# A Vector product moved behind a weight step, and the column split of one down-projection matmul regrouped

## The reference

```
x = x + 0.5 * rms(swiglu(rms(x)))                       # ffn1, d_ff = 2816
x = x + rms(mix(diff_attention, ssd) @ w_mix_out)       # two branches, gated
x = x + rms(cross_attention(x, mem))
x = x + 0.5 * rms(swiglu(rms(x)))                       # ffn2, d_ff = 2816
# second block
proj = rms(x) @ w_in_2
v, x1, x2 = split(short_conv(hy_in))
for o, gate in enumerate((x1, x2)):                     # hyena: long convolution by FFT
    zc = gate * (irfft(rfft(zc) * k_spec[o]) + bias * zc)
attn = softmax(q k / sqrt(96)) v                        # 8 heads, no mask
x = x + (g_hy * (zc * silu(z_hy)) @ w_hy_out + g_at * (attn * silu(z_attn)) @ w_attn_out) @ w_out
```

## Time and profile before

| | |
|---|---|
| runs of the kernel before | 1109.22, 1107.14, 1108.89 us |
| median | 1108.89 us |
| profiled execution | 1109.22 us, of which the span is 1107.4 us |
| PE busy | 1091.7 us, 99% of the span, 8538 matmuls |
| DVE busy | 792.8 us, 72% |
| ACT busy | 590.7 us, 53% |
| PEclk, all 40 slices | 9, which is 90% or more |

### The profile page before, as it was taken

One profiled execution on the slowest core, in us unless ns is written; L12 is line 12 of the kernel. 1 busy time (PEld: TensorE's weight loads), 2 busy tenths in 40 slices (PEclk: granted clock), 3 DMA queues, 4 the chain that ended last, 5 costly groups with the idle time before them and its releaser, 6 DMA issues.

```text
span 1107.4 us, 21002 instructions
## 1 busy us (share of the span) xinstructions
PE 1091.7 (99%) x8538; PEld 1035.5 (94%) x8538; DVE 792.8 (72%) x1112; ACT 590.7 (53%) x844; POOL 0.2 (0%) x4
## 2 busy tenths in 40 slices
PE   9999999999999999999999999999999999999998
PEld 8999999999999999999999888899999798999998
DVE  6765556858898977777777867665555686997774
ACT  5444444567764335587744555454444575655561
POOL 0000000000000000000000000000000000000000
PEclk9999999999999999999999999999999999999999
DMA  8665555455444336444555434365556445543341
GB/s 302 245 224 189 201 183 189 184 191 178 167 157 148 97 132 205 158 152 153 190 175 182 171 115 160 101 224 192 189 187 206 136 167 200 187 152 118 112 153 38
DMA packets 29137, 188.59 MB, mean 170 GB/s; under 512 B 3496, under 2 KB 4809, under 8 KB 7370
## 3 DMA queue, kind: packets, MB, share of 16 engines
q1 hardware_dynamic: 26592, 181.42, 47.4%
q10 hardware_dynamic: 2474, 6.15, 1.7%
HBM read 186.50 MB, written 1.05 MB: 169 GB/s over the span
## 4 chain that ended last, share of the span: by engine, by line
PE 80%; DVE 13%; ACT 4%; issue 2%; DMA 1%; ACTq 0%; SPq 0%; DVEq 0%
PE bank L508 23%; PE bank L510 23%; PE bank L509 23%; DVE sb_w_lo L1990 3%; PE bank L589 2%; DVE sb_ssd_conv L2213 2%; ACT sb_w_hi L1304 2%; PE bank L833 1%; PE bank L715 1%; PE bank L663 1%; DVE sb_hT_lo L2067 1%; DMA sb_w_raw<-in_w 1%; PE bank L1151 1%; PE bank L1050 0%; PE bank L978 0%
## 5 line engine op out<-in xcount | busy, mean ns | idle before, releaser
L1990 DVE TENSOR_TENSOR sb_w_lo<-sb_w_raw,sb_w_hi 128x2048 fp32r<-128x2048 f32 x169 | 386.4, 2290 | 153.2 <-ACT sb_w_hi L1304 153.0
L508 PE MATMUL bank<-sb_hT_hi,sb_w_hi 128*128 128x256 f32 x1560 | 440.3, 282 | 2.0 <-DVE sb_hT_lo L2067 1.0
L509 PE MATMUL bank<-sb_hT_lo,sb_w_hi 128*128 128x256 f32 x1560 | 433.1, 278 | 0.0
L510 PE MATMUL bank<-sb_hT_hi,sb_w_lo 128*128 128x256 f32 x1560 | 433.0, 278 | 0.0
L1304 ACT ACTIVATE sb_w_hi<-sb_w_raw 128x2048 fp32r<-128x2048 f32 x169 | 322.7, 1910 | 35.5 <-PE bank L510 34.1
L508 PEld LDWEIGHTS bank<-sb_hT_hi,sb_w_hi 128*128 128x128 f32 x1560 | 293.4, 188 | 6.0 <-issue 4.3
L509 PEld LDWEIGHTS bank<-sb_hT_lo,sb_w_hi 128*128 128x128 f32 x1560 | 292.9, 188 | 1.5 <-issue 1.2
L510 PEld LDWEIGHTS bank<-sb_hT_hi,sb_w_lo 128*128 128x128 f32 x1560 | 292.5, 188 | 0.0
L1358 ACT ACTIVATE sb_ffn_gate<-sb_ffn_gate 128x256 f32<-128x256 f32 x44 | 18.4, 418 | 137.2 <-DVE sb_ffn_gate L2082 137.1
L508 PE MATMUL bank<-sb_w_hi,sb_hT_hi 128*128 128x256 f32 x256 | 73.4, 287 | 0.6 <-DVE sb_hT_lo L2742 0.2
L510 PE MATMUL bank<-sb_w_hi,sb_hT_lo 128*128 128x256 f32 x256 | 71.3, 279 | 0.0
(11 more groups left out here) (437 smaller groups left out, 1801.5 us busy)
## 6 DMA issues: line engine op xcount, KB each, us to landing
sb_w_raw<-in_w SPq DMA_DIRECT2D x169, 1024.0 KB, 5.0
sb_x<-in_x SPq DMA_DIRECT2D x2, 512.0 KB, 4.4
sb_w_raw<-in_w SPq DMA_DIRECT2D x4, 256.0 KB, 6.5
sb_w_raw<-in_w SPq DMA_DIRECT2D x2, 512.0 KB, 7.7
sb_mem_xn<-in_mem ACTq DMA_DIRECT2D x1, 1024.0 KB, 7.1
sb_post_g<-in_ffn_post_g ACTq DMA_DIRECT2D x2, 512.0 KB, 4.5
sb_decay<-in_c_decay ACTq DMA_DIRECT2D x1, 768.0 KB, 4.4
out<-sb_x SPq DMA_DIRECT2D x3, 256.0 KB, 2.1
```

The source lines that it names most:

```text
L508: pe.matmul(o, a_hi, b_hi, start=first, stop=False)
L509: pe.matmul(o, a_hi, b_lo, start=False, stop=False)
L510: return pe.matmul(o, a_lo, b_hi, start=False, stop=last)
L1990: tt(w_lo[b % STAGES][:], w_raw[b % RING][:], f32(w_hi[b % STAGES][:]), ALU.subtract).then_inc(w_lo_in, 1)
```

## The change

The entry of `LAST_DOWN` for the eight looped down blocks of ffn2 changes from two pieces of 256 columns in all three products to pieces of 320 and 192 columns in the third product alone. And on DVE `hyena_product(0, 1)` moves from the tail of step 0, where it stood between `softmax_rows(0)` and `low_after`, to the head of step 1, which is behind the `low_after` of step 0 and ahead of `softmax_rows(1)`.

```diff
 LAST_DOWN = {1: (((256, 256), False), ((256, 256), True), ((384, 128), False)),
-             2: (((256, 256), True), ((256, 256), True), ((448, 64), False))}
+             2: (((256, 256), True), ((320, 192), False), ((448, 64), False))}
...
                 if i == 0:
                     hyena_product(0, 0)
                     centred_conv(4)
+                elif i == 1:
+                    hyena_product(0, 1)
                 elif i == 3:
...
                     softmax_rows(i)
                 if i in (4, 6, 8):
                     at_low(c)
-                if i == 0:
-                    hyena_product(0, 1)
-                elif i == 1:
+                if i == 1:
                     centred_conv(5)
```

## The result

| | before | after |
|---|---|---|
| median | 1109.22 us (5 runs, 1107.14 to 1110.63) | 1115.08 us (5 runs, 1113.50 to 1116.57) |
| ratio after / before, 95% interval | | 1.0054, 1.0039 to 1.0069 |
| profiled execution, its span | 1109.22 us, 1107.4 us | 1114.64 us, 1112.8 us |

A forecast was written before the change was run, and what follows sets the result against it. PE, busy 99% of the span, was taken as the bound. The wait's +2.78 us and the split's -0.1 made +2.7: 1111.6 us on the median, put at 1111.5 for new runs, range 1109.7 to 1112.8 for 8 in 10.

The forecast's parts named there:

- Part two, the wait: Product moved behind step 0's `w_lo` on DVE: PE waits at the transposes of head 1, +2.78 us (2.4 to 3.15).
- six steps: Chain from `softmax_rows(0)`: DVE idles 3.15 us for `w_hi`, row maximum and ACT's exponentials shift 3.15, PE ends 2.78 us late.
- second wait: Further PE wait behind the transposes, at `hyena_back(0)`: worth 0 to 0.37 us, taken as nothing.
- the step after the sixth: `hyena_unfold(0)` now ends at 1012.94, PE wants its second half at 1013.02: fits by 0.08 us, less the hop.
- Part one, the split: ffn2's looped down blocks, third product in 320 + 192: 0.01 us saved a turn, eight turns -0.1 us (-0.2 to +0.2).
- The four shapes: Down-block splits in the trace: all three 256 + 256, third alone 256 + 256, 384 + 128 or 448 + 64; excess 0.03 to 0.11 us.
- The excess of 0.05: Old split, all three products 256 + 256: 1.18 us from first L715 matmul to fifth up-block start, against ideally 1.13.
- The rival on the clock: PE's clock falls to 1.2 GHz behind the gap at the transposes: 2.7 us more, 1114.3 us; chance 0.06.
- the wait of 1.89 us: PE's longest idle time in the trace before, which left the clock at 1.00; cited against the clock falling.
- half a weight block at half rate: Clock rival's price: 24 matmuls of 256 columns behind the gap take 0.227 us instead of 0.113, costing 2.7 us more.

## Why the prediction was wrong in size

**Part two, the wait: right.** Its six steps hold one by one. 2.78 us was forecast; at full clock the move alone costs 2.94 by its mean and 2.5 in its profile, and in the profile after it was 3.10. There DVE stood some 0.36 us later against PE than the forecast had it (`w_lo` at 997.64 is 1.14 behind it, PE just ahead of the place 0.78), which would make up the difference. No second wait came in `hyena_back(0)`, as the step after the sixth says.

**Part one, the split: the price at the cut was right, and the sum that followed from it was wrong.** The step that failed is the one that closed the account at the fifth matmul: "Nothing hides it, since PE is the bound in the loop, and nothing else depends on it." What depended on it was the pitch of the 96 matmuls behind. The four shapes were each read for 1.2 us, and each of them happens to be followed by the fast pitch, so no view of the shapes at the cut could tell. But the trace had it. The excess of 0.05 that the prediction gives the old cut was this very thing in part: from 752.24 to 752.71 the matmuls of 256 columns take 0.118 each, and 0.113 from there on. Whoever had asked where in the whole trace 256 columns take 0.118 would have found two states, 136 of 452 stretches in the slow one, and a loop of 768 matmuls in the fast one that the change could push over. That risk is 768 x 0.0045 = 3.5 us, less what the first matmuls behind each cut paid before, and it had no place among the rivals. It was forecast at -0.1 and is +3.1 in the trace, +3.5 in the runs of the split alone.

The Trainium skill ("TensorE: Matmul & The Clock Gate", section "Back-to-back issue gap") gives an isolated matmul N / 2.4 + 2.5 ns, by an estimate 109 ns for 256 columns. The matmuls here are not isolated, each has its own weight load; in a long stream the traces have 113.3 or 117.8 ns, and no run here shows 109.

**The rival on the clock: the mechanism was real, its chance and price were not.** It had a chance of 0.06 and +2.7 us. It came in 9 of 14 executions that had this wait, and cost 1.5 us. The argument against it, the wait of 1.89 us that leaves the clock at 1.00, was one case, and with three operations moved, where the new wait is 1.22 us, 4 of 11 executions lost the clock. The forecast needed both numbers: how often, and that the half clock lasts 3.4 us (PE was busy for 3.29 of them), where it had taken half a weight block at half rate, 5.4 us.

**The sum.** Split +3.5, move +2.9 at full clock and 5 of 8 times 1.5 for the clock make +7.4; the kernel after is 5.9 above before by the medians of the result, 6.8 by the mean of all runs of before. The parts exceed the whole by 0.6 to 1.5 us. The scatter of single runs (before 1106.0 to 1111.5) and the pitches that change by chance are of that size; whether one effect is smaller when they stand together was not settled.

**The result's place in the range.** 1115.08 lies 2.3 us above the upper end, 1112.8. That the kernel is slower by over 0.2% was foreseen for a reason, the wait, that covers half of the result; of the other half the clock stood among the rivals, and the pitch nowhere.

## What to carry to other kernels

When a stream of equal matmuls bounds the kernel, read its pitch in many places before pricing an edit of it: if there are two, an edit is worth what it does to the pitch of all that follows, not what it costs itself. And where a wait is laid in front of PE, price the clock with it, as a chance times its cost; here the row maxima ahead of the product, in place of behind it, left PE waits of 0.95 and 0.43 us in place of 2.3, and the clock stayed full.

## What the runs showed of the hardware

- A stream of 256-column matmuls, each with its weight load, runs at 0.1133 or at 0.1178 us a matmul and keeps its pitch for over 80 matmuls. In the two loops, a last piece of 256 or 128 columns at the end of the down block set the fast one in every profile (but for ffn1's first looped turn, where a wait for `w_lo` at 54 us comes between), and one of 192, 320 or 512 columns the slow one. Inside a slow stream 128 + 128 set the fast one in three places of four, 192 + 64 in none of four. Elsewhere it differs between profiles for the same stretch. What lies behind it is not shown.
- In the profile of the kernel after, PE's granted clock fell to half (1.2 GHz) for 3.4 us, right behind a wait of 2.9 us, at a cost of 1.5 us. By the mean clock, 5 of 8 executions of that kernel lost it, 4 of 6 of the move alone (wait 2.3 us) and 4 of 11 with three operations moved (1.2 us); in these two no profile shows where. Those at 0.998 took 1.5, 1.6 and 2.6 us longer than the others of their kernel. In 14 executions in which matmuls filled the gap no loss is seen, in eight of them by their times too.
